# A fourth expert body, for 65 to 96 tokens, in the expert loop of a hybrid GLA, convolution and mixture-of-experts step

## The reference

```python
def run_block(args):
    e, idx, wt = args
    xb = hf[idx]
    hb = jax.nn.silu(xb @ w_g[e]) * (xb @ w_u[e])
    return ((hb @ w_d[e]) * wt[:, None]).astype(hf.dtype)
```

## Time and profile before

| | |
|---|---|
| runs | 1722.47, 1720.03, 1720.81 us |
| profiled execution | 1719.95 us, span 1718.1 us |
| PE busy | 1433.8 us, 83% of the span |
| VectorE, ScalarE, GpSimd busy | 26%, 7%, 3% |
| PE's granted clock, mean | 0.898 of full speed |
| chain that ended last | PE 55%, DMA 38% |
| moved by DMA | 585 MB, mean 340 GB/s |

### The profile page before, as it was taken

How to read it: one execution, slowest core, us unless ns; L and a number is a source line. 1 busy time by engine, 2 the same in 40 slices (tenths; PEclk the granted TensorE clock), 3 DMA queues, 4 the chain that set the end, 5 groups by cost and what they waited for, 6 DMA issues and landing times.

```text
span 1718.1 us, 17166 instructions
## 1 busy us (share of the span) xinstructions
PE 1433.8 (83%) x6847; PEld 621.6 (36%) x6848; DVE 443.7 (26%) x874; ACT 127.1 (7%) x199; POOL 48.5 (3%) x23
## 2 busy tenths in 40 slices
PE   2889999999879996569867768997999966899973
PEld 0434343334444453124313313431445421445422
DVE  0210029920230243311312112222202312201315
ACT  0001200200410000000100000000000000000000
POOL 1000000100000002400000000000000000000000
PEclk8899999999969997679979879998899978899977
DMA  9995666676846188999999999999996999997894
GB/s 352 373 397 193 239 250 247 250 272 255 329 181 235 68 298 356 401 411 417 418 414 416 419 416 415 417 418 413 417 419 242 392 417 413 417 418 282 349 414 170
DMA packets 139461, 584.98 MB, mean 340 GB/s; under 512 B 13491, under 2 KB 15627, under 8 KB 112796
## 3 DMA queue, kind: packets, MB, share of 16 engines
q1 hardware_dynamic: 129408, 562.07, 83.1%
q10 hardware_dynamic: 10012, 22.37, 3.5%
HBM read 581.19 MB, written 3.21 MB: 340 GB/s over the span
## 4 chain that ended last, share of the span: by engine, by line
PE 55%; DMA 38%; DVE 3%; issue 2%; SPq 2%; ACT 1%; DVEq 0%; POOL 0%; ACTq 0%
PE bank L670 20%; DMA late<-in_w_e_down_dram 13%; DMA ring<-in_w_e_up_dram 12%; PE bank L965 12%; DMA ring<-in_w_e_gate_dram 9%; PE bank L978 6%; PE bank L942 4%; PE bank L906 3%; PE bank L629 3%; DMA ring<-in_w_in_dram 2%; DMA ring<-in_w_mod_dram 1%; SPq L280 1%; DMA late<-in_w_e_up_dram 1%; PE bank L1039 1%; PE bank L805 1%
## 5 line engine op out<-in xcount | busy, mean ns | idle before, releaser
L965 PE MATMUL bank<-ring,work 128*32 128x512 f32 (+2 forms) x1536 | 324.0, 708 | 106.7 <-DMA ring<-in_w_e_up_dram 43.5
L670 PE MATMUL bank<-ring,hT 128*128 128x512 f32 x768 | 344.8, 605 | 7.6 <-DMA ring<-in_w_in_dram 4.7
L670 PEld LDWEIGHTS bank<-ring,hT 128*128 128x128 f32 x768 | 145.1, 193 | 203.7 <-issue 199.6
L965 PEld LDWEIGHTS bank<-ring,work 128*32 128x32 f32 (+2 forms) x1536 | 84.2, 133 | 327.8 <-issue 166.1
L942 PEld LDWEIGHTS bank<-work,arena 128*128 128x128 f32 x1088 | 136.9, 208 | 23.7 <-issue 19.2
L942 PE MATMUL bank<-work,arena 128*128 128x128 f32 x1088 | 141.7, 293 | 4.4 <-DVE work L1355 4.4
L1129 DVE SCALAR_TENSOR_TENSOR arena<-work,late,arena 128x256 f32<-128x256 f32 x240 | 95.3, 477 | 0.0
L978 PE MATMUL bank<-ring,work 128*32 128x512 f32 (+2 forms) x512 | 89.1, 595 | 0.0
L965 PE MATMUL bank<-late,work 128*32 128x512 f32 (+2 forms) x256 | 58.2, 762 | 21.1 <-DMA late<-in_w_e_gate_dram 11.7
L965 PE MATMUL bank<-hT,work 128*32 128x512 f32 (+2 forms) x256 | 57.9, 759 | 21.4 <-DMA hT<-in_w_e_gate_dram 10.8
L1367 DVE COPY work<-bank 128x512 f32<-128x512 f32 x68 | 47.0, 691 | 83.6 <-PE bank L942 83.6
(11 more groups left out here) (233 smaller groups left out, 800.3 us busy)
## 6 DMA issues: line engine op xcount, KB each, us to landing
ring<-in_w_mod_dram SPq DMA_DIRECT2D x96, 1024.0 KB, 7.1
ring<-in_w_e_gate_dram SPq DMA_DIRECT2D x96, 1024.0 KB, 18.6
ring<-in_w_e_up_dram SPq DMA_DIRECT2D x96, 1024.0 KB, 18.6
ring<-in_w_e_down_dram SPq DMA_DIRECT2D x64, 1024.0 KB, 19.0
ring<-in_w_in_dram SPq DMA_DIRECT2D x40, 1024.0 KB, 5.0
hT<-in_w_e_down_dram SPq DMA_DIRECT2D x32, 1024.0 KB, 21.6
late<-in_w_e_down_dram SPq DMA_DIRECT2D x32, 1024.0 KB, 24.2
ring<-in_w_out_dram SPq DMA_DIRECT2D x16, 1024.0 KB, 7.2
```

What stands on the lines that cost most here:

```text
L670: last = mm(ps[bank[k]][:, :], hT[:, kt, g * P:(g + 1) * P], ring[:, n % SLOTS, i * 1024 + hf * BANK:i * 1024 + (hf + 1) * BANK], start=(k ...
L965: last = mm(ps[bank][at:at + rows, :], XT[:, kt, 0:rows], buffer(i % DEEP)[:, k * 1024 + hf * BANK:k * 1024 + (hf + 1) * BANK], start=(i < ...
```

## The change

The `size` in `steps` becomes 1 to 4, and a body `three` for 65 to 96 tokens stands between `two` and `four` in all three loops. On PE each unit is run first with 64-column tiles for tokens 0 to 63 and then with 32-column tiles for tokens 64 to 95, so twice as many matmuls per unit as any other body. The first 64 tokens are treated as in `two`, the last 32 as in `one` (folded; `fold_pair` is cut out of `one` for that). In the combine, for each of the 8 banks, a matmul over 64 rows opens the bank and one over 32 rows closes it. The gates of tokens 64 to 95 have their own matrices (`wsel3`, `wselT3`, from places `place3`), made by VectorE at the start of the step. The table gets one more row (the place of the gates) and its last operations are rearranged: seven linked operations in place of four ahead of `tab_rdy`. The semaphores `bk_a`, `bk_v` and `bk_hTp` count to 3 per step in place of 2, in every body. Steps of body `one`, `two` and of more than 96 tokens compute what they did.

```diff
@@ for_steps @@
-        def for_steps(eng, one, two, four):
+        def for_steps(eng, one, two, three, four):
...
-                    size = eng.value_load(steps[0:1, 1, bass.ds(t, 1)], min_val=1, max_val=3)
+                    size = eng.value_load(steps[0:1, 1, bass.ds(t, 1)], min_val=1, max_val=4)
                     with eng.If(size < 2):
                         one(t)
                     with eng.If(size == 2):
                         two(t)
-                    with eng.If(size > 2):
+                    with eng.If(size == 3):
+                        three(t)
+                    with eng.If(size > 3):
                         four(t)
@@ ScalarE @@
+            def three(t):
+                up_done(t)
+                nc.scalar.activation(hs[:, 0, :], ps[0][:, :], ACT.Silu).then_inc(bk_a, 1)
+                nc.scalar.copy(hs[:, 1, :], ps[2][:, :]).then_inc(bk_a, 1)
+                act.wait_ge(bk_hTp, t * 3 + 2)
+                nc.scalar.activation(hs[:, 1, 0:256], ps[2][:, 0:256], ACT.Silu).then_inc(bk_a, 1)
+                down_done(t)
+                nc.scalar.copy(yf[:, 0:BANK], ps[0][:, :]).then_inc(bk_y, 1)
+                nc.scalar.copy(yf[:, 2 * BANK:3 * BANK], ps[2][:, :]).then_inc(bk_y, 1)
@@ TensorE @@
-            def up(t, rows, place):
+            def up(t, *parts, rest=False):
 
                 pe.wait_ge(st_xv, t * 4 + 4)
                 for i in range(16):
                     if i < 2:
-                        pe.wait_ge(st_add, t * 8 + 2 * (i + 1))
+                        pe.wait_ge(st_add, t * 8 + (4 if rest else 2 * (i + 1)))
                     if i == 5:
                         pe.wait_ge(st_add, t * 8 + 8)
                         for g in range(G):
                             last = tr(ps[4][:, g * P:(g + 1) * P], wsel[:, g, :], ident)
+                        if rest:
+                            pe.wait_ge(bk_v, t * 3 + 1)
+                            for g in range(G):
+                                last = tr(ps[4][:, (2 + g) * P:(3 + g) * P], wsel3[:, g, :], ident)
                         last.then_inc(st_wTp, 1)
...
                     unit_in(t, i)
-                    for k in range(2):
-                        kt = 2 * (i // 2) + k
-                        for hf in range(2):
-                            bank, at, chains = place(i % 2, k, hf)
-                            last = mm(ps[bank][at:at + rows, :], XT[:, kt, 0:rows],
-                                      buffer(i % DEEP)[:, k * 1024 + hf * BANK:k * 1024 + (hf + 1) * BANK],
-                                      start=(i < 2 and k < chains), stop=(i >= 14 and k >= 2 - chains))
+                    for c0, rows, place in parts:
+                        for k in range(2):
+                            kt = 2 * (i // 2) + k
+                            for hf in range(2):
+                                bank, at, chains = place(i % 2, k, hf)
+                                last = mm(ps[bank][at:at + rows, :], XT[:, kt, c0:c0 + rows],
+                                          buffer(i % DEEP)[:, k * 1024 + hf * BANK:k * 1024 + (hf + 1) * BANK],
+                                          start=(i < 2 and k < chains), stop=(i >= 14 and k >= 2 - chains))
                     last.then_inc(used, 1)
...
-            def down(t, rows, weights, place):
+            def down(t, *parts):
...
                     unit_in(t, 16 + i)
-                    for q in range(NQ):
-                        bank, at = place(q)
-                        last = mm(ps[bank][at:at + rows, :], weights(i),
-                                  buffer((16 + i) % DEEP)[:, q * BANK:(q + 1) * BANK],
-                                  start=(i == 0), stop=(i == FT - 1))
+                    for rows, weights, place in parts:
+                        for q in range(NQ):
+                            bank, at = place(q)
+                            last = mm(ps[bank][at:at + rows, :], weights(i),
+                                      buffer((16 + i) % DEEP)[:, q * BANK:(q + 1) * BANK],
+                                      start=(i == 0), stop=(i == FT - 1))
                     last.then_inc(used, 1)
...
+            def fold_pair(a, b, gate, product, count):
+
+                pe.wait_ge(bk_a, gate)
+                for c in range(4):
+                    last = mm(ps[2][:, c * 64:(c + 1) * 64], a[:, c * P:(c + 1) * P], fold, start=True, stop=True)
+                last.then_inc(bk_hTp, 1)
+                pe.wait_ge(bk_v, product)
+                for c in range(4):
+                    last = mm(ps[3][:, c * 64:(c + 1) * 64], b[:, c * P:(c + 1) * P], fold, start=True, stop=True)
+                last.then_inc(bk_hTp, count)
...
+            def three(t):
+                up(t, (0, TWO, lambda s, k, hf: (s, 64 * hf, 1)),
+                   (TWO, ONE, lambda s, k, hf: (2 + s, 64 * k + 32 * hf, 2)), rest=True)
+                gather_half(t + 1, 0)
+                pe.wait_ge(bk_v, t * 3 + 2)
+                for c in range(4):
+                    last = tr(ps[0][:, c * P:(c + 1) * P], hh[:, 0, c * P:(c + 1) * P], ident)
+                last.then_inc(bk_hTp, 1)
+                fold_pair(hs[:, 1, :], hh[:, 1, :], t * 3 + 2, t * 3 + 3, 1)
+                gather_half(t + 1, 1)
+                down(t, (TWO, lambda i: hT8[:, i % 4, TWO * (i // 4):TWO * (i // 4 + 1)], lambda q: (q // 2, TWO * (q % 2))),
+                     (ONE, lambda i: hTs3[:, i % 4, ONE * (i // 4):ONE * (i // 4 + 1)], lambda q: (2, ONE * q)))
+                pe.wait_ge(bk_y, t * 4 + 4)
+                pe.wait_ge(st_xv, t * 4 + 8)
+                for j in range(G * NQ):
+                    g, q = divmod(j, NQ)
+                    r = slice(TWO * (q % 2), TWO * (q % 2) + TWO)
+                    mm(ps[j][:, :], wselT[r, g, :], yf[r, (q // 2) * BANK:(q // 2 + 1) * BANK], start=True, stop=False)
+                    r = slice(ONE * q, ONE * q + ONE)
+                    mm(ps[j][:, :], wselT3[r, g, :], yf[r, 2 * BANK:3 * BANK], start=False, stop=True).then_inc(st_cmb, 1)
@@ VectorE @@
-            link(v.tensor_scalar(over, by_step(cnt), ONE + 0.5, None, ALU.is_gt))
-            link(v.scalar_tensor_tensor(over, by_step(cnt), TWO + 0.5, over, ALU.is_gt, ALU.add))
-            link(v.tensor_scalar(steps[:, 1, 0:NE], rt[:, 10, 0:NE], 1.0, None, ALU.add))
-            v.tensor_scalar(steps[:, 2, 0:NE], rt[:, 10, 0:NE], float(P), None, ALU.mult).then_inc(tab_rdy, 1)
+            col = lambda i: rt[:, i, 0:NE].rearrange("p (e g) -> p e g", g=NGRP)
+            link(v.tensor_scalar(col(10), by_step(cnt), ONE + 0.5, None, ALU.is_gt))
+            link(v.scalar_tensor_tensor(col(11), by_step(cnt), TWO + 0.5, col(10), ALU.is_gt, ALU.add))
+            link(v.scalar_tensor_tensor(col(12), by_step(cnt), THREE + 0.5, col(10), ALU.is_gt, ALU.add))
+            link(v.scalar_tensor_tensor(col(10), by_step(cnt), THREE + 0.5, col(11), ALU.is_gt, ALU.add))
+            link(v.tensor_scalar(steps[:, 2, 0:NE], rt[:, 11, 0:NE], float(P), None, ALU.mult))
+            link(v.tensor_scalar(steps[:, 4, 0:NE], rt[:, 12, 0:NE], float(P), None, ALU.mult))
+            v.tensor_scalar(steps[:, 1, 0:NE], rt[:, 10, 0:NE], 1.0, None, ALU.add).then_inc(tab_rdy, 1)
...
+            def three(t):
+                e = dve.value_load(steps[0:1, 0, bass.ds(t, 1)], min_val=0, max_val=NE - 1)
+                weigh(wsel3, e, place3).then_inc(bk_v, 1)
+                dve.wait_ge(st_wTp, t + 1)
+                v.tensor_copy(wselT3, ps[4][:, 256:512].rearrange("p (g t) -> p g t", g=G))
+                weights_next(t)
...
```

More of the change, by code:

```diff
@@ L34 @@
 CAP = 128
-ONE, TWO = 32, 64
+ONE, TWO, THREE = 32, 64, 96
 CONV_W = 1024
@@ L173, in hybrid_step @@
         places = part(work, 9216, 4 * P)
+        place3 = part(work, 10560, P)
+        hTs3 = part(work, 8704, 4, 2 * ONE)
+        wselT3 = part(arena, 9728, G, P)
+        wsel3 = part(arena, 9984, G, P)
         fold = part(work, 10496, TWO)
@@ L584, in four @@
                 for hf in range(2):
[L585 removed]
+                    nc.scalar.activation(hs[:, hf, :], ps[hf][:, :], ACT.Silu).then_inc(bk_a, 1 + hf)
                 down_done(t)
@@ L588, in four @@
                     nc.scalar.copy(yf[:, q * BANK:(q + 1) * BANK], ps[2 + q][:, :]).then_inc(bk_y, 1)
-            for_steps(act, one, two, four)
+            for_steps(act, one, two, three, four)
             for g in range(G):
@@ L983, in one @@
             def one(t):
-                up(t, ONE, lambda s, k, hf: (s, 64 * k + 32 * hf, 2))
+                up(t, (0, ONE, lambda s, k, hf: (s, 64 * k + 32 * hf, 2)))
                 gather_half(t + 1, 0)
-                pe.wait_ge(bk_a, t * 2 + 1)
-                for c in range(4):
-                    last = mm(ps[2][:, c * 64:(c + 1) * 64], hs[:, 0, c * P:(c + 1) * P], fold, start=True, stop=True)
-                last.then_inc(bk_hTp, 1)
-                pe.wait_ge(bk_v, t * 2 + 2)
-                for c in range(4):
```

(22 more changed lines are left out.)

62 lines of the change are left out of this document (39 added, 23 removed).

## The result

The changed kernel takes 1934.71 us (median of 4 runs, 1932.73 to 1935.94), the kernel before 1720.42 in the runs beside it: a ratio of 1.1249, 95% interval 1.123 to 1.1268. The forecast was 1910, in a range of 1820 to 1965. The profiled execution has a span of 1934.1 us, 216.0 more than before.

A forecast was written before the change was run, and what follows sets the result against it. Middle-size expert steps were taken as DMA-bound at the weights' pace, 60.4 us a step. Waits for PE code, summed by stretches with the new body, add 190 to 1720: 1910 us, range 1820 to 1965.

The forecast's parts named there:

- The code of the loop: PE's loop grows from seven to eleven code pieces; about eight held, oldest replaced, so jumps wait; some 180 packets.
- The waits at each boundary: Code waits on PE between steps, by body sizes: one to one 4, one to four 7, one to three 6.
- rival (1): Each code piece has a fixed place, so pieces 4 and 5 stay; three waits one to one; 1840 us; chance 0.27.
- Rivals (2) and (3): All eleven pieces fit: (2) only the first pass pays, 1725, chance 0.08; (3) tile switches also free, 1709, chance 0.05.
- Rival (4): PE also waits inside bodies because the fetch ahead comes late: 1960 and above; chance 0.10 with other slow mishaps.
- Price of a wait: A PE jump to absent code costs 6.6 us while weights stream, 5 (an estimate) once the stream stands.
- T5 to T8: From step 5's last weight landing to step 8's, holding two steps of body two: 181.2 us becomes 223.4.
- One to one: A body-one step after another: 67.4 us in place of 60.4, six such steps giving +42.
- the 6.0: Time in us from a step's last weight landing to PE's first matmul of the next step, code waits excluded.
- the 35.0: Time in us from PE's first matmul to the step's last weight landing: 1.9 + 2.9 + 30.2.
- The combine: Body three's combine at step 13, its 64-row and 32-row matmuls alternating: 16.1 us in place of 7.1.
- The body as a gain: Body three in place of body four at step 13: -3.6 us, or -19.6 were tile switches free.

The follow-up runs named there:

- experiment 1: Changed kernel with the new size's bound set to 64, so body three stays in the code but never runs: 1929.5 us, ratio 1.1241.
- experiment 3: Kernel before plus a fourth PE body of 20 transposes that never runs, loop ending at instruction 1,804: 1904.93 us, ratio 1.1091.
- experiment 4: Changed kernel with nested tests: size < 3 encloses bodies one and two, size > 2 encloses three and four: 1738.16 us, ratio 1.012.
- experiments 2: Kernel before plus a fourth PE body of 6 transposes that never runs, loop ending at instruction 1,776: 1720.75 us, ratio 1.0012.
- experiments 7: Changed kernel with grouped combine, body three's units in pairs, and a test tree: one, then a block of four and three, then two: 1729.32 us.
- experiment 10: Changed kernel without body one (two runs up to 64 tokens), four and three in a block behind two, combine grouped, units paired: 1735.77 us.
- experiment 11: Changed kernel with nested tests, grouped combine and body three's units in pairs: 1722.75 us, ratio 1.0027.
- the nested versions: Changed kernel with tests nested, one and two under one test, three and four under another: 1738.16 us alone, 1726.17 us with grouped combine.
- experiment 8: Changed kernel with only bodies two and three in the loops, step 9 leaving out 26 of its 122 tokens: 1763.41 us, ratio 1.026.
- experiment 5: Changed kernel with body three's combine grouped: eight 64-row matmuls first, then eight 32-row ones: 1922.7 us, ratio 1.1178.

## Why the prediction was right, point by point

**The code of the loop.** Right, and shown: the loss is there without the new body (1), comes with 28 instructions that never run (3), and goes when the same code is entered in fewer pieces (4). The number eight, taken from seven pieces held and one fetched ahead, is now bounded from both sides: repeated passes of eight pieces keep them (experiments 2 and 4), a pass of nine loses every piece that it jumps to (3). The forecast of some 180 packets met 181. The Trainium skill, "Runtime: NRT & Kernel Launch", Instruction fetch mechanics, gives 2048 instructions in blocks of 256: the trace agrees, eight pieces kept and nine not. That the first in is the first out, as it also says, holds for passes that always go the same way, and does not explain experiments 7 and 10.

**The waits at each boundary.** Four from one to one, as counted. That piece 4 is absent each time (L267, median 6.1 us) speaks against rival (1), which had it stay, and experiment 4 excludes that rival. Rivals (2) and (3), that all fits, fall with the 181 packets. Rival (4), waits inside the bodies, falls with the line of the waits: the 363 us stand in front of first units, and inside the bodies PE shows next to none.

**Price of a wait.** 6.6 was a little low: the first of a row takes 6.1, those behind it 7.4, 7.4 and 6.9, less 0.2 each as a usual test: 27.0 for four in place of 26.4. Without the stream I took 5 as an estimate. With the DMA all but idle the waits of the changed kernel measure 3.4 to 5.0. T5 to T8, where eight waits were put at 5, came to 223.5 against 223.4, and this is in part luck: four of the eight came while weights still moved (6.1 to 7.5), the other four took 3.4 to 4.6, and their mean is 5.4.

**One to one** is the first term that was mis-sized: 67.4 forecast, 69.2 to 70.8 measured, over six steps about 15 us. First matmul at T3 + 34.3 (991.12 less 956.78) in place of 32.4, and from there to T4 36.5 in place of 35.0. Of the first 1.9, 0.6 are the waits; the rest is the combine ahead of them, 3.97 in place of 2.58, at a granted clock of 0.57 (959.6 to 963.6), which was 1.00 in the kernel before. The first units behind the waits ran at 0.76 (991.0 to 996.8), which the sum counted for the first of them alone; how much of the 1.5 behind the first matmul this makes was not taken apart. So what was mis-sized is the 6.0 in the main, read in a step that PE ended at the full clock, and the 35.0.

**The combine** is the second: 16.1 forecast, 28.5 measured. My sum of the switches (16 changes at 0.15, half an excursion each) holds as long as the clock does (1.05 for two matmuls in the trace, against 2 x 0.505); that the granted clock would fall to 0.50 in it was missing. It is 12.4 of the 13.0 by which T12 to T14 is longer than forecast.

**The body as a gain.** -3.6 forecast; as written it loses 8.4 against body four with the same code around it (110.7 less 102.3, experiment 1). The -3.6 was right in the units (2.88), and the combine's 12.4 more make it +8.8. By the Trainium skill, "TensorEngine Tiling (Array Packing)", Key Properties, a change of tiling mode drains the engine. The trace agrees in so far as a change has a price: four units take 10.95 with half the changes and 11.52 with all, 0.14 a change. That the ends of the sum were so far apart (-3.6 and -19.6) was fair: grouped and paired, body three does gain, 7 us from T12 to T15 in experiment 11 (195.2 against 202.2).

**Together** +190 forecast, +216 measured: +15 one to one, +13 at T12 to T14 (the combine), +2 at T0 to T2, -4 at the four.

**What stays open:** which piece gives way. Cyclic passes are explained by the oldest going first, but after step 9 the nested versions fetched pieces again that I had taken as held, and one wait took 12.07 us (L261 above). In experiment 4 the code queue moved five packets around step 9 (1225 to 1331), where by "oldest first" three pieces were missing (8, 9 and 0). In experiment 10 the jump to piece 8 behind step 9 waited 5.4 us, though only three packets of code (pieces 9, 4 and 5) had been moved since the first pass fetched piece 8. So a store of eight that drops its oldest piece is not the whole rule. The count of pieces says when a repeated pass is held; it does not foretell the waits around a rare step.

## What to carry to other kernels

Before a body is added to a loop with jumps, count the pieces of code that the commonest pass enters, with the one fetched ahead behind each jump. If the trace shows no more packets of the code queue after the first pass, the loop is held, and a few instructions can end that. Keep what runs rarely behind one test, so that the common pass jumps over it once. Group matmuls by tile form, and look at the granted clock of the stretch before the durations of a new order are summed.

## What the runs showed of the hardware

A loop of 1,776 instructions on PE ran at 1720.75 us and one of 1,804 at 1904.93, none of the added instructions running: the border lies within these 28 instructions. A jump to a piece that has only just been asked for waits too (5.7 us at L268 in experiment 3). And alternating matmuls of 64 and of 32 rows, 100% busy by the profile, ran into a granted clock of 0.50 when the form changed at every matmul (after, experiment 8), where the same matmuls in two groups had 1.00 (experiment 5).
